# Preparing beats in turns: one-hot units, dots and choice steps on VectorE, gate products and row sums on TensorE, ring slots freed one by one

## The reference

```python
s = jnp.einsum('thpd,hpnd->thpn', qf, sub_keys)        # 8 heads, 2 x 128 keys
sv, si = lax.top_k(s, PEER_TOPK)                       # 16 of 128, for each key half
cand = sv[:, :, 0, :, None] + sv[:, :, 1, None, :]     # 256 candidates a head
top_s, pos = lax.top_k(cand, PEER_TOPK)                # 16 experts a head
gate = jax.nn.softmax(top_s, axis=-1)
act = jax.nn.gelu(jnp.einsum('td,thkd->thk', xb, u_tab[ib]), approximate=False)
out = jnp.einsum('thk,thkd->td', gb * act, v_tab[ib])
```

## Time and profile before

| | us |
|---|---|
| median of 3 runs | 4371.06 |
| the runs | 4370.55, 4371.06, 4422.45 |
| the profiled execution | 4379.46 |
| its span, first to last instruction | 4377.7 |
| preparing beats, by its timeline | 1715.6 to 2408.2 |
| mean granted clock of PE | 0.899 of full |

### The profile page before, as it was taken

How to read it: one execution, slowest core, us unless ns; L and a number is a source line. 1 busy time by engine, 2 the same in 40 slices (tenths; PEclk the granted TensorE clock), 3 DMA queues, 4 the chain that set the end, 5 groups by cost and what they waited for, 6 DMA issues and landing times.

```text
span 4377.7 us, 32776 instructions
## 1 busy us (share of the span) xinstructions
PE 3614.1 (83%) x9773; PEld 1830.1 (42%) x9773; DVE 2902.0 (66%) x6214; ACT 1030.3 (24%) x2646; POOL 1046.9 (24%) x950
## 2 busy tenths in 40 slices
PE   7885999866787875666754798999989999999998
PEld 4344444323433432243433344444444444444443
DVE  2537887657467867877777566676767667755565
ACT  1312212462412111144546111111111111111111
POOL 0100322222122222222110232333323323333231
PEclk9987999988899887777775899999999999999999
DMA  5342766656577787866651999999989989999997
GB/s 202 144 152 102 291 224 244 233 209 244 191 304 286 277 320 283 324 269 259 252 219 67 346 366 357 363 378 365 396 345 368 362 342 375 367 377 364 367 373 280
DMA packets 254840, 1268.06 MB, mean 290 GB/s; under 512 B 24596, under 2 KB 75028, under 8 KB 135622
## 3 DMA queue, kind: packets, MB, share of 16 engines
q0 software_dynamic: 131504, 958.53, 56.9%
q1 hardware_dynamic: 121720, 302.19, 18.6%
q10 hardware_dynamic: 1440, 5.24, 0.3%
HBM read 1216.30 MB, written 49.58 MB: 289 GB/s over the span
## 4 chain that ended last, share of the span: by engine, by line
PE 57%; DMA 18%; DVE 15%; issue 4%; ACT 3%; SPq 1%; POOL 0%; DVEq 0%; ACTq 0%
PE bank L1056 13%; DMA arena<-in_ut 11%; PE wide L1068 8%; PE bank L1016 8%; PE bank L984 5%; PE bank L1068 4%; PE bank L820 4%; DMA ring_e<-in_uv,idx 3%; PE bank L843 3%; PE wide L775 3%; PE bank L967 3%; PE bank L1036 2%; DMA arena<-in_w_q 2%; PE wide L1004 2%; DVE ring_e L1614 2%
## 5 line engine op out<-in xcount | busy, mean ns | idle before, releaser
L1056 PE MATMUL bank<-arena 128*128 128x384 f32 x2048 | 725.7, 510 | 141.2 <-DMA arena<-in_ut 141.1
L721 POOL DMA_INDIRECT arena<-in_uv,idx x384 | 428.5, 1116 | 1241.9 <-PE bank L1016 630.8
L1674 DVE CUSTOM_DVE_ANT_0 arena<-arena,h2e 128x1024 f32<-128x1024 f32 x384 | 461.7, 1222 | 377.9 <-DMA arena<-in_uv,idx 377.6
L1056 PEld LDWEIGHTS bank<-arena 128*128 128x128 f32 x2048 | 405.9, 200 | 472.2 <-DMA arena<-in_ut 151.3
L698 POOL DMA_INDIRECT ring_e<-in_uv,idx x256 | 305.8, 1195 | 1088.5 <-PE wide L775 526.2
L1674 DVE CUSTOM_DVE_ANT_0 ring_e<-ring_e,h2e 128x1024 f32<-128x1024 f32 x256 | 307.9, 1223 | 247.4 <-DMA ring_e<-in_uv,idx 246.8
L1068 PE MATMUL wide<-arena 128*128 128x512 f32 x1024 | 460.3, 592 | 0.0
L721 POOL DMA_INDIRECT ring_e<-in_uv,idx x256 | 289.3, 1130 | 675.1 <-PE bank L1016 348.3
L1349 ACT ACTIVATE small<-small 128x4 f32<-128x4 f32 x160 | 32.9, 205 | 1729.8 <-DVE small L1674 1729.7
L1614 DVE CUSTOM_DVE_ANT_0 ring_e<-ring_e,h2e 128x1024 f32<-128x1024 f32 x256 | 307.9, 1222 | 177.1 <-DMA ring_e<-in_uv,idx 176.5
L984 PE MATMUL bank<-arena 128*128 128x512 f32 (+1 forms) x768 | 302.9, 551 | 50.1 <-DMA arena<-in_w_q 47.6
(11 more groups left out here) (238 smaller groups left out, 4764.7 us busy)
## 6 DMA issues: line engine op xcount, KB each, us to landing
arena<-in_ut SPq DMA_DIRECT2D x128, 512.0 KB
arena<-in_uv SPq DMA_DIRECT2D x128, 512.0 KB, 8.8
arena<-in_w_q SPq DMA_DIRECT2D x48, 512.0 KB, 11.1
spread_d<-arena SPq DMA_DIRECT2D x12, 2048.0 KB, 6.7
arena<-spread_d SPq DMA_DIRECT2D x32, 768.0 KB
ring_e<-in_w_mod POOLq DMA_DIRECT2D x8, 2048.0 KB, 7.8
arena<-in_w_cols SPq DMA_DIRECT2D x24, 512.0 KB, 3.6
arena<-in_x SPq DMA_DIRECT2D x20, 512.0 KB, 3.7
```

What stands on the lines that cost most here:

```text
L721: pool.indirect_dma_start(out=ring[r], out_offset=None, in_=a["uv"], in_offset=bass.IndirectOffsetOnAxis(ap=idx[kept(t)][:, k:k + 1], axis ...
L1056: ins = pe.matmul(s_bank[:, 0:NC], lhsT=utb[i % URING][:, k * P:(k + 1) * P], rhs=H2T[1][:, k, P:P + NC], start=(k == 0), stop=(k == KD - 1))
L1674: dve.tensor_tensor_reduce(out=ring[r][:, 0:D], in0=ring[r][:, 0:D], in1=h2b[kept(t)], scale=1.0, scalar=0.0, op0=ALU.mult, op1=ALU.add, a ...
```

## The change

Nothing is computed otherwise. The order within the preparing beats changes on three engines, and ring slots are marked used one by one:

- PE: `sums_full(g)` becomes `sum_full(n)`, one row, which marks its slot. A beat is four times a unit and a row sum, unit first; the transposed choice comes ahead of them.
- ACT: emptying and one-hots of the four units come first, then the Gelu, the exponential of a choice, the diagonals.
- DVE: a beat is four times (one-hots of a unit, one dot), with one choice step behind each of the first three dots. Results of finished tiles and any fourth choice step follow, then the weights. One-hots no longer stand at the beat's end.
- `a_used` counts rows, in `sum_full` and in `sums_half`; a gather waits for the row of its own slot, in the expert stage too. The other waits on `a_used` are renumbered to the same rows as before.

```diff
@@ -709,7 +709,7 @@
                 if k == 0:
                     pool.wait_ge(S["idx_ready"].sem, t + 1)
                 if n >= RING:
-                    pool.wait_ge(*S["a_used"].at((n - RING) // GROUP))
+                    pool.wait_ge(*S["a_used"].at(n - RING))
                     if n - RING >= SLOTS:
                         pool.wait_ge(*S["a_half"].at(n - RING))
                 elif r < ERING:
@@ -994,17 +994,16 @@
                         if hp < HP:
                             early(s, f"qf{j}", hp)
 
-            def sums_full(g):
-
-                for n in range(g * GROUP, (g + 1) * GROUP):
-                    pe.wait_ge(*S["a_diag"].at(n))
-                    if n == 0:
-                        pe.wait_ge(*S["acc_read"].at(0))
-                    for h in range(2):
-                        ins = pe.matmul(wide[0][:, h * 512:(h + 1) * 512], lhsT=diag[n % 8],
-                                        rhs=ring[n % RING][:, D + h * 512:D + (h + 1) * 512],
-                                        start=(n == 0), stop=(n == SLOTS - 1), skip_group_check=True)
-                ins.then_inc(*S["a_used"].mark(g))
+            def sum_full(n):
+
+                pe.wait_ge(*S["a_diag"].at(n))
+                if n == 0:
+                    pe.wait_ge(*S["acc_read"].at(0))
+                for h in range(2):
+                    ins = pe.matmul(wide[0][:, h * 512:(h + 1) * 512], lhsT=diag[n % 8],
+                                    rhs=ring[n % RING][:, D + h * 512:D + (h + 1) * 512],
+                                    start=(n == 0), stop=(n == SLOTS - 1), skip_group_check=True)
+                ins.then_inc(*S["a_used"].mark(n))
 
             def sums_half(g):
 
@@ -1037,13 +1036,14 @@
                 full(ins, ("G", t, u))
 
             for b in range(BEATS):
-                if 1 <= b <= GROUPS_A:
-                    sums_full(b - 1)
                 for t in C_TILES:
                     if b == choice_beat(t):
                         turn_choice(t)
-                for t, u in units_at(b):
-                    spread(t, u)
+                for j in range(GROUP):
+                    for t, u in units_at(b)[j:j + 1]:
+                        spread(t, u)
+                    if 1 <= b <= GROUPS_A:
+                        sum_full((b - 1) * GROUP + j)
             for key in units[-4:]:
                 pe.wait_ge(*emptied(key))
 
@@ -1352,7 +1352,7 @@
 
                 act.wait_ge(*S["a_weight"].at(g))
                 if g >= 2:
-                    act.wait_ge(*S["a_used"].at(g - 2))
+                    act.wait_ge(*S["a_used"].at((g - 1) * GROUP - 1))
                 for n in range(g * GROUP, (g + 1) * GROUP):
                     j = n % 8
                     act.activation(diag[j], ident[:], ACT.Copy, scale=wts[:, j:j + 1]).then_inc(*S["a_diag"].mark(n))
@@ -1376,21 +1376,22 @@
             act.wait_ge(*S["front_done"].at(NT - 1))
             act.wait_ge(*S["bank_full"].at(("hT1", NT - 1)))
             for b in range(BEATS):
+                for t, u in units_at(b):
+                    empty_spread(t, u)
+                    if u + 2 < UNITS:
+                        ones_for(t, u + 2)
                 if b < GROUPS_A:
                     gelu_group(b)
-                    diag_group(b)
                 for t, q in picks_at(PICK_BEATS, b):
                     if q == HP + PH:
                         pick_exp(t)
+                if b < GROUPS_A:
+                    diag_group(b)
                 for t in C_TILES:
                     if b == choice_beat(t):
                         empty_choice(t)
                         for u in range(2):
                             ones_for(t, u)
-                for t, u in units_at(b):
-                    empty_spread(t, u)
-                    if u + 2 < UNITS:
-                        ones_for(t, u + 2)
                 for t, at in ((0, 0), (1, 3), (2, GROUPS_A + 4)):
                     if b == at:
                         root(t)
@@ -1661,14 +1662,14 @@
                 dve.scalar_tensor_tensor(out=x, in0=x, scalar=frs[:, r:r + 1], in1=finalb,
                                          op0=ALU.mult, op1=ALU.mult).then_inc(*S["y_ready"].mark(t))
 
-            def dots_of(g):
-
-                for n in range(g * GROUP, (g + 1) * GROUP):
+            def dots_of(g, j=None):
+
+                for n in range(g * GROUP, (g + 1) * GROUP) if j is None else (g * GROUP + j,):
                     t, k = slot_of(n)
                     r, j = n % RING, n % 8
                     if k == 0:
                         dve.wait_ge(*S[f"h2_in{kept(t)}"].at(t))
-                    if k % GROUP == 0 and g >= 2:
+                    if n % GROUP == 0 and g >= 2:
                         dve.wait_ge(*S["a_gelu"].at(g - 2))
                     dve.wait_ge(*landed[r].at(n))
                     dve.tensor_tensor_reduce(out=ring[r][:, 0:D], in0=ring[r][:, 0:D], in1=h2b[kept(t)], scale=1.0,
@@ -1995,21 +1996,29 @@
 
             dve.wait_ge(*S["dot_e"].at(2 * SLOTS - 1))
             for b in range(BEATS):
-                if b < GROUPS_A:
-                    dots_of(b)
+                steps = list(picks_at(PICK_BEATS, b))
+                for j in range(GROUP):
+                    for t, u in units_at(b)[j:j + 1]:
+                        if u + 2 < UNITS:
+                            ones_for(t, u + 2)
+                    if b < GROUPS_A:
+                        dots_of(b, j)
+                    if j < GROUP - 1:
+                        for t, q in steps[j:j + 1]:
+                            pick_step(t, q)
                 if b == 2:
                     dve.wait_ge(*S["y_sum"].at(0))
                     dve.wait_ge(*used_e(2 * SLOTS - 1))
                     gate_sums(1, [wide[1][:, h * 512:(h + 1) * 512] for h in range(2)])
                     residual(1)
                 if b == GROUPS_A + 3:
-                    dve.wait_ge(*S["a_used"].at(GROUPS_A - 1))
+                    dve.wait_ge(*S["a_used"].at(SLOTS - 1))
                     gate_sums(2, [wide[0][:, h * 512:(h + 1) * 512] for h in range(2)])
                     residual(2)
                 for t, at in ((0, 1), (1, 4), (2, GROUPS_A + 5)):
                     if b == at:
                         normalised(t)
-                for t, q in picks_at(PICK_BEATS, b):
+                for t, q in steps[GROUP - 1:]:
                     pick_step(t, q)
                 if b < GROUPS_A:
                     weights_of(b)
@@ -2017,14 +2026,11 @@
                     if b == choice_beat(t):
                         for u in range(2):
                             ones_for(t, u)
-                for t, u in units_at(b):
-                    if u + 2 < UNITS:
-                        ones_for(t, u + 2)
 
             for i in range(ETILES):
                 for t in A_TILES[1:-1]:
                     if i == tile_end(t) + 1:
-                        dve.wait_ge(*S["a_used"].at(tile_end(t) + GROUPS_A - 1))
+                        dve.wait_ge(*S["a_used"].at((tile_end(t) + GROUPS_A) * GROUP - 1))
                         dve.wait_ge(*S["a_half"].at((tile_end(t) + GROUPS_A) * GROUP - 1))
                         gate_sums(t, [half_bank[:], acc_half[A_TILES.index(t) % 2]])
                     if i == tile_end(t) + 2:
@@ -2039,7 +2045,7 @@
                     pick_step(t, q)
                 weigh(i)
             last = A_TILES[-1]
-            dve.wait_ge(*S["a_used"].at(len(A_TILES) * GROUPS_A - 1))
+            dve.wait_ge(*S["a_used"].at(len(A_TILES) * SLOTS - 1))
             dve.wait_ge(*S["a_half"].at(len(A_TILES) * SLOTS - 1))
             gate_sums(last, [half_bank[:], acc_half[A_TILES.index(last) % 2]])
             residual(last)
```

## The result

The changed kernel takes 4131.75 us (median of 4 runs, 4127.35 to 4148.02) against 4370.81 for the kernel before: ratio 0.9452, 95% interval 0.9416 to 0.9488. The profiled execution spans 4134.1 us.

A forecast was written before the change was run, and what follows sets the result against it. In the preparing beats no engine was full and DVE waited for PE; in the expert stage PE and DMA were near their limits. Terms summed to -148 us, giving 4231 profiled, 4223 on the median's scale; range 4160 to 4305.

The forecast's parts named there:

- beats 0 to 10: First preparing beats: slots freed row by row and choice steps filling waits give 150 us, a gain of 15.
- 11 to 18: Preparing beats with units: DVE work plus 1.6 us a beat gives 131.8 us from 163.5, a gain of 31.7.
- 19 and 20: Two preparing beats: DVE work 25.06 plus 2.0 us gives 27.1 from 35.3, a gain of 8.2.
- 21 to 30: Preparing beats, eight with units: DVE work plus hand-overs gives 160.3 us from 197.1, a gain of 36.8.
- 31 to 38: Last preparing beats, almost no dots: DVE work plus 1.4 us a beat gives 110 from 131.5, a gain of 21.5.
- late by 0 to 1.4: Unit beats: PE's slow clock after idling makes the second unit late for DVE; 0.75 us a beat taken.
- The hand-over: Between preparing and expert stage: earlier last store lets the first expert load issue sooner, a gain of 15 us.
- The expert stage: Dense pass over 128 expert tiles: gathers go 2.6 us earlier after stalls, a gain of 20 us, 50 at best.
- C: Expert stage stalls go, PE restarts less slowly and the first beats reach their floor: 4165 us, chance 0.13.
- A: Unit beats: PE stays at 1.2 GHz, the beat is as slow as before; 4281 us, chance 0.10.
- B: Expert stage: earlier gathers take bandwidth from expert loads and PE waits more; up to 4576 us, chance 0.10.
- D: Packed preparing beats: rows land late as DMA takes over as bound, expert stage gains nothing; 4272 us, chance 0.12.

The follow-up runs named there:

- Run 5: Changed kernel with all choice steps of a beat behind its four dots again, one-hots still between the dots: 4205.92 us.
- run 7: Changed kernel plus ten added 128-column products into unused PSUM in PE's wait of each unit beat up to 31: 4132.32 us.
- runs 3 and 4: First: changed kernel with group release in the preparing beats, 4135.49 us. Second: kernel before with release by row everywhere, old orders, 4249.58 us.
- run 1: Changed kernel with the four ring slots of a group released together again in the expert stage: 4239.75 us.
- run 2: Kernel before with release by row in the expert stage only, preparing beats left as they were: 4265.28 us.
- run 6: Changed kernel, but in the expert stage a group's first three slots are released together at its third row sum: 4214.7 us.
- run 9: Changed kernel with a third buffer for u tiles, loaded one step earlier: 4085.03 us.
- run 8: Kernel before with a third buffer for u tiles, loaded one step earlier, release still by group: 4214.59 us.
- run 11: Kernel before with 30 of the 32 gate-matrix loads left out in the expert stage, so stale gates are used: 4274.99 us.

## Why the prediction was wrong

**The preparing beats: right, by their terms, with some luck in the sum.** Against the earlier trace rows: beats 0 to 10 gave 18.1 us (15 forecast), 11 to 18 34.6 (31.7), 19 and 20 4.5 (8.2), 21 to 30 36.1 (36.8), 31 to 38 25.9 (21.5). The terms themselves were met where they can be read: the Gelu's 0.27 us, and a wait of DVE for the second unit of 1.18 us where "late by 0 to 1.4" stood; over beats 11 to 18 DVE waits 6.2 us for units, 0.78 a beat where I took 0.75, and stands 1.5 us a beat in all where I took 1.6. Run 5 shows the choice steps at work as cover, run 7 the clock as the cause of the slow first row. Not met: beats 19 and 20, where half the gain came. DVE had 2.0 us for hand-overs there and stood 4.8: 1.8 for a tile that ScalarE's L1317 writes, as before, 1.8 for a unit product and 0.8 for the Gelu; its work was 0.9 more. And what I wrote of beats 0 to 10, that release by row matters there, is half the story (runs 3 and 4). Their 18.1 us are close to the 15 by luck: the 11.85 us for the key scores stood in no term, and the waits for rows went entirely.

**The hand-over: right.** 17.6 us for 15. The last store now starts at 2288.28, before the first gather at 2295.56. PE waits 11.27 us for the first u tile, 22.38 before, and then the gathers' landing sets the start, as the chain of the kernel after says:

```profile
2299.28 18.16 DMA ring_e<-in_uv,idx
```

**The expert stage: the step that failed.** It was "19 x 2.6 = 50 at best, nothing at worst. I take -20." The direction and the place were right (runs 1 and 2), the size was 115. Three things were wrong in this term.

First, its own row was misread. "19 stalls" is 141.1 us over one stall's 7.35; the row says 33 waits, one of them the 22.4 us of the hand-over. With 33 the same sum gives 86.

Second, it had nothing for PE's slow time behind a stall. From the windows, before: 1895 us with PE busy 1783.97, so idle 111; after: 1779 with 1750.89, idle 28. Of the 116 us between the windows 83 are idle time and 33 are PE working at a better clock on the same products (0.97, then 0.99). C had 15 for it, the forecast none.

Third, it took the number of stalls as given. It was not: 49 steps of over 14.2 us before, 18 after, 49 in run 1, 46 in run 6, 24 in run 2, 2 in run 9. The trace of the kernel before shows what a stall does. The stretch around 3198.00, in windows: PE's wait and most of the scores, the end of the scores with the four row sums (3205.90 to 3209.34), and the 6 us after:

```profile
3190.00:3204.00 14.00, 6.65 (x13) 3.32 (x12) 9.50 (x20) 1.48 (x5) 0.94 (x1) 0.63 1.01 418
3204.00:3210.00 6.00, 6.00 (x17) 3.01 (x16) 5.83 (x14) 0.49 (x1) 0.23 (x1) 1.00 0.11 44
3210.00:3216.00 6.00, 6.00 (x16) 2.85 (x15) 0.80 (x3) 0.00 (x0) 3.73 (x4) 1.00 0.71 249
```

While PE stands for the u tile, DMA is full (1.01). It runs dry afterwards (0.11), when PE is busy again: all gathers have landed, and the next goes at 3209.77, behind the four row sums. Release by row moves it 2.6 us forward. Counted from the packets in slices of 1 us, DMA's share is under 0.5 in 131 us of the stage before, in 121 in run 1, 94 in run 6, 39 in run 2, 24 in the kernel after and none in run 8. In the kernel before these slices form 28 stretches of 4.7 us in the mean, and 27 of them lie in a step whose scores had waited for the u tile.

That such a stretch leads to the next stall is worked out, not shown by itself. Neither resource has time to spare. PE needs 126 x 13.75 = 1732.5 us, and DMA 691.76 MB at the 400 GB/s of run 8, 1729 us. So what DMA does not move in 4.7 us it cannot catch up, and a later u tile is late by it, most often the one behind a gate load. Each stall so prepares the next, and a shorter dry stretch makes stalls fewer. The same loop opens at another place in run 8 (the tile a step earlier) and at a third in run 11 (the load ahead of it left out): 101.5 us in run 2, 105.9 in run 11, 156.5 in run 8.

A second number in the same paragraph comes close: DMA share 0.94, so 0.06 x 1895 = 114 us "that could be won". The match with 115 is luck. Run 8 won 156.5 us, with a share of 1.01, so 114 was no bound. The distance from PE's own pace holds: 1889.6 - 1732.5 = 157 before, 42 left after, 1 in run 8.

**The rivals.** A did not occur: the granted clock rose from 0.74 to 0.87 in beats 11 to 18; PE recovers in each beat after its first row (3.64 us, then 1.88). The Trainium skill's rule (TensorE: Matmul & The Clock Gate, What's actually happening), that throttled is the default and activity releases it, agrees with this. B did not occur: the wait for u fell. In run 1 and in the kernel after the loads are issued at the same points, and PE waited less for them with the earlier gathers, 39.2 us against 127.6. The Trainium skill's turns between queues (DMA: Bandwidth & Descriptors, Queues, rings and completion order) concern the gathers (q0 in the trace) against the loads (q1), and do not explain run 11: all of SP's loads, the gate load and the u load with them, go by q1 (162.83 MB of the stage before). I had put the weight on the wrong competitor. D did not occur; in beats 0 to 30 of the kernel after DVE waits for no gathered row. C was the one on the right side ("the stalls of the expert stage go"), and it too stood at 4165, with 65 us for a stage that gave 115.

## What to carry over

Where two resources are both near full and each waits for the other through a short buffer, the number of today's stalls times the lead is too little: the stalls feed each other, and a lead of 2.6 us in a step of 13.75 was worth 5 to 6% of the stage. Take the distance from the pace at which the fuller one never stands and never slows down; here that was PE's 13.75 us a step, not the idle share of DMA. Ask first which transfer is late and give that one a buffer more: one buffer (4 KB per partition) was worth 157 us, the release by row 101 to 115. In a rotation of short pieces over three engines, sum the busiest engine's work per turn, add the hand-overs that lose their cover, and the result holds within 5% for the four long stretches here; for the two beats 19 and 20 it was 12% short. And look at the first turn by itself: a piece moved forward can meet data that is not there yet.

## What the runs showed of the hardware

The gate load, 768 KB in rows of 512 bytes, took 22.0 us from issue to landing in the expert stage of the kernel after, and the u load, 512 KB in rows of 4 KB, 10.4:

```profile
arena<-in_ut SPq DMA_DIRECT2D x125, 512.0 KB, 10.4
arena<-spread_d SPq DMA_DIRECT2D x30, 768.0 KB, 22.0
```

3.4% of the stage's bytes (24 of 709 MB) go with two thirds of the time that its long steps lose (107 of 155 us, run 11). PE and DMA can both be full for 1720 us: 13.75 us a step at 400 GB/s (runs 8 and 9). In the expert stage of the kernel before their idle times never met: in slices of 1 us DMA's share was 1.01 in the mean while PE stood, and in no slice with a share under 0.5 did PE stand. One semaphore mark per row instead of one per four cost PE nothing that is seen: from the first of four half row sums to the next product are 3.43 us before (2456.09 to 2459.52) and 3.44 after (2609.79 to 2613.23). And PE was at 1.2 GHz after standing for 2.73 us in beat 13 (granted clock 0.51), where I had allowed for a beat in which it stays fast.
